# Two RMS norms by chunks of 128 tokens, x in four transfers, and rotation angles behind the next weight split

## The chip, the cores and the metric

The kernel runs on one core of a Trainium2 chip. Its time is the device time of one execution in microseconds; a kernel's time is the median of its runs. The engines are named as in the profile: PE (TensorE), DVE (VectorE), ACT (ScalarE), POOL (GpSimd) and SP (SyncE, which here only issues transfers). Each has its own instruction stream, in program order, and they are held together by semaphores.

## The reference, cut to what matters

Two blocks of a model are applied to 512 tokens of width 1024 in float32. The part that the change touches:

```python
def _rmsnorm(x, g):
    y = xf * lax.rsqrt(jnp.mean(xf * xf, axis=-1, keepdims=True) + NORM_EPS)
    return (y * g.astype(jnp.float32)).astype(x.dtype)

# first block
u = _rmsnorm(h, norm_mix_g[l]);  z = einsum('bsd,dn->bsn', u, w_in[l])      # norm 0
h = h + einsum('bsd,de->bse', merged, w_out[l])
m = _rmsnorm(h, norm_mlp_g[l]);  hid = square(relu(m @ w_mlp_in[l]))        # norm 1
h = h + hid @ w_mlp_out[l];      x = _rmsnorm(h, norm_final_g)

# second block
cos, sin = rope_tables(positions, HEAD_DIM)                                 # rotation angles
lower_bounds = cumsum(softmax(hgrn_lb_logits)) - lb_w[0]
h = rmsnorm(x, norm_mix) * (1.0 + scale_m) + shift_m                        # norm 2
x = x + gate_m * hybrid_mixer(h, cos, sin, ...)
h = rmsnorm(x, norm_ffn) * (1.0 + scale_f) + shift_f
x = x + gate_f * hierarchical_moe(h, ...)
return rmsnorm(x, norm_final)
```

## The kernel before, in words

Tokens lie on the 128 partitions in four chunks (`X[:, c, :]`, c = 0 to 3, 1024 elements each). The large products want the other layout, features on the partitions, so each of the norms 0, 1 and 2 ends in a transposition. Each float32 operand is split into a high and a low part, and one product is three matmuls of 512 columns (`three`, L342 to L344).

Weights come as units of 1 MB in one ring of two buffers (`RAW`, `WH`, `WL`). For each unit, SP issues the load (L519), ACT rounds it to the high part (`split_hi`, L323; it may only begin when PE has finished the unit that used the buffer), DVE subtracts to get the low part (`split_lo`, L327), and PE multiplies. So unit n+1 is split while PE works on unit n. Unit 0 is split outside the loop, on ACT at L671 and on DVE at L951.

A norm before the change goes in steps for all four chunks together. ACT squares each chunk and sums along it (`squares`, L269, a square and the read of the sum); POOL then adds epsilon and raises to -1/2 for the four columns at once (`norm_pool`, L285 and L287); ACT scales chunks 0 and 1 (L274) and DVE chunks 2 and 3 (`norm_scale`, L302); PE transposes (`norm_pe`, L296), eight groups k of 128 features with four transpositions each, into PSUM banks 4 to 7, so that groups 4 to 7 wait for DVE to be done with groups 0 to 3; per group ACT writes the high part `UH` (L279, in norm 2 L281) and DVE the low part `UL` (L310, in norm 2 L312 and L314). After that come PE's products: in norms 0 and 1 the first unit is a `feature` product, which goes over k from 0 to 7 for its first half and then again for its second; each k of the first half of norm 1's unit waits for `UL` of that k.

Norm 1 follows the output projection (units F0 to G0-1). DVE adds its last results chunk by chunk to `X` (L1094), and ACT's squares follow these additions.

After norm 2, ACT computes an exponential for the lower bounds (L788) and then waits for DVE's rotation angles before it computes the sine (L791) and the cosine (L792). Only after these does ACT reach `split_hi` of unit H0+1. DVE has the lower bounds (L1147 to L1150) and the angles (L1153 to L1165) behind the norm and ahead of `split_lo` of unit H0+1. Unit H0 has been split long before.

The last third of the kernel, the experts, is fed by 1 MB loads on SP's queue, each of which waits for a step of the computation that frees its buffer.

Of the kernel before, what the change touches and what calls it, by code (L numbers as in the profile page):

```python
# [81 lines left out]
def build(nc, t):  # L82

    ctx = ExitStack()
    with ctx:
# [178 lines left out]
        def squares(act, j, added, count):  # L264

            for c in range(NC):
                if added is not None:
                    act.wait_ge(added, count + c + 1)
                act.activation(XN[:, c, :], X[:, c, :], ACT.Square, accum_out=SS[:, c:c + 1]).then_inc(norm_sq, 1)  # L269

        def norm_act(act, j, chunks, gain=None):
            act.wait_ge(norm_rs, 2 * j + 2)
            for c in chunks:
                act.activation(XN[:, c, :], X[:, c, :], ACT.Copy, scale=SS[:, 4 + c:5 + c]).then_inc(norm_xn, 1)  # L274
            for k in range(KD):
                act.wait_ge(norm_tr, KD * j + k + 1)
                src = PS[:, 4 + k % 4, :]
                if gain is not None:
                    act.activation(UH[:, k, :], src, ACT.Copy, scale=COLS[:, gain + k:gain + k + 1]).then_inc(norm_hi, 1)  # L279
                else:  # L280
                    act.activation(UH[:, k, :], src, ACT.Identity, scale=MODC[:, 8 + k:9 + k], bias=MODC[:, k:k + 1]).then_inc(norm_hi, 1)  # L281

        def norm_pool(pool, j):
            pool.wait_ge(norm_sq, NC * j + NC)
            pool.tensor_scalar(SS[:, 0:4], SS[:, 0:4], 1.0 / D, EPS, ALU.mult, ALU.add).then_inc(norm_rs, 1)  # L285
            pool.wait_ge(norm_rs, 2 * j + 1)
            pool.tensor_tensor(SS[:, 4:8], SS[:, 0:4], COLS[:, 60:64], ALU.pow).then_inc(norm_rs, 1)  # L287

# [10 lines left out]
        def norm_scale(dve, j, chunks):  # L299
            dve.wait_ge(norm_rs, 2 * j + 2)  # L300
            for c in chunks:
                dve.tensor_scalar(XN[:, c, :], X[:, c, :], SS[:, 4 + c:5 + c], None, ALU.mult).then_inc(norm_xn, 1)  # L302

        def norm_dve(dve, j, gain=None):

            for k in range(KD):
                dve.wait_ge(norm_hi, KD * j + k + 1)
                src, hi = PS[:, 4 + k % 4, :], UH[:, k, :].bitcast(F32)
# [113 lines left out]
        y_out, yc_in = [sem("y_out0"), sem("y_out1")], [sem(f"yc_in{c}") for c in range(NC)]  # L422
# [244 lines left out]
        def _(act):  # L667
            act.wait_ge(const_in, 16 * NCONST)
# [3 lines left out]
            norm_act(act, 0, (0, 1), 0)  # L672
# [94 lines left out]
            norm_act(act, 1, (0, 1), 16)  # L767
# [19 lines left out]
            act.wait_ge(lb, 1)  # L787
            act.activation(LBS[:, 3:6], LBS[:, 0:3], ACT.Exp).then_inc(lb, 1)  # L788

            act.wait_ge(trig, 2)  # L790
            act.activation(SINS, TRG[:, 2, :], ACT.Sin, scale=COLS[:, 53:54]).then_inc(trig, 1)  # L791
            act.activation(COS, TRG[:, 3, :], ACT.Sin).then_inc(trig, 1)  # L792
            for n in range(H0, I0):
                split_hi(act, 0, n // 2, n % 2)
                if n % 2:
                    h = (n - H0) // 2
                    act.wait_ge(unit_done, n + 1)
                    for c in (0, 2):
                        act.activation(V2[:, c:c + 2, HALF * h:HALF * h + HALF], PS[:, 4 * h + c:4 * h + c + 2, :], ACT.Copy).then_inc(z2_out, 1)
# [104 lines left out]
            def h2_row(c):  # L904
                act.wait_ge(norm_rs, 2 * 3 + 2 * c + 2)
# [40 lines left out]
        def _(dve):  # L946
            link = Link(dve, dve_link)
            dve.wait_ge(const_in, 16 * NCONST)
            norm_scale(dve, 0, (2, 3))
# [147 lines left out]
            norm_scale(dve, 1, (2, 3))  # L1097
# [48 lines left out]
            dve.wait_ge(lb, 2)  # L1146
            link(dve.reciprocal(LBS[:, 6:9], LBS[:, 3:6]))  # L1147
            link(dve.tensor_tensor(LBS[:, 3:6], LBS[:, 3:6], LBS[:, 6:9], ALU.mult))
            link(dve.tensor_tensor(LBS[:, 0:3], LBS[:, 3:6], LBS[:, 3:6], ALU.subtract))
            dve.tensor_scalar(LBS[:, 9:12], LBS[:, 0:3], -1.0, 1.0, ALU.mult, ALU.add).then_inc(lb, 1)  # L1150

            dve.wait_ge(pos_in, 32)
            link(dve.tensor_copy(TRG[:, 1, :], TRG[:, 0, :].bitcast(I32)))  # L1153
            link(dve.tensor_scalar(TRG[:, 1, :], TRG[:, 1, :], COLS[:, 52:53], None, ALU.mult))
            for k, quarter in ((2, 0.0), (3, 0.25)):
                if k == 2:
                    dve.wait_ge(x2_d, 4)
                link(dve.tensor_scalar(TRG[:, 0, :].bitcast(I32), TRG[:, 1, :], 1.0 / TWO_PI, quarter, ALU.mult, ALU.add))
                link(dve.tensor_copy(RT, TRG[:, 0, :].bitcast(I32)))
                link(dve.scalar_tensor_tensor(TRG[:, k, :], RT, -TURN[0], TRG[:, 1, :], ALU.mult, ALU.add))  # L1160
                link(dve.scalar_tensor_tensor(TRG[:, k, :], RT, -TURN[1], TRG[:, k, :], ALU.mult, ALU.add))
                link(dve.scalar_tensor_tensor(TRG[:, k, :], RT, -TURN[2], TRG[:, k, :], ALU.mult, ALU.add))
                if quarter:
                    link(dve.tensor_scalar(TRG[:, k, :], TRG[:, k, :], TWO_PI / 4, None, ALU.add))
                dve.tensor_scalar(TRG[:, k, :], TRG[:, k, :], PI_IN, -PI_IN, ALU.min, ALU.max).then_inc(trig, 1)  # L1165
# [344 lines left out]
        def _(pool):  # L1510
            link = Link(pool, pool_link)
            pool.wait_ge(const_in, 16 * NCONST)
            norm_pool(pool, 0)
# [47 lines left out]
            norm_pool(pool, 1)  # L1561
# [66 lines left out]
            def rstd(x):  # L1628
# [3 lines left out]
                pool.wait_ge(norm_rs, 2 * 3 + 2 * x + 1)  # L1632
# [61 lines left out]
        def _(pe):  # L1694
            pe.wait_ge(const_in, 16 * NCONST)
            norm_pe(pe, 0)
# [158 lines left out]
            norm_pe(pe, 1)  # L1855
# [607 lines left out]
```

## Time and profile before

| | |
|---|---|
| median of 3 runs (lowest, highest) | 1414.85 us (1409.91, 1417.54) |
| the profiled execution's own time | 1410.52 us |
| its span | 1408.7 us |
| PE busy | 1295.4 us (92%) |
| DVE, ACT, POOL busy | 643.8, 386.4, 264.6 us |
| mean granted clock of PE | 0.953 |

The span goes from the first instruction to the last. An engine's busy time is the sum over its instructions; matmuls are pipelined, so a matmul's own duration (0.39 us) is longer than the distance to the next (0.23 us). A releaser is the instruction whose semaphore ended a wait. In the rows below a time such as 382.59 is microseconds from the start of the span.

### The profile page before, as it was taken

The page shows a single profiled execution, that of the slowest core. Times are in us where ns is not written, and L with a number is a line of the kernel's source. Part 1 is how long each engine was busy: PE and PEld are TensorE (multiplying, and loading weights), DVE is VectorE, ACT ScalarE, POOL GpSimd, SP SyncE. Part 2 cuts the span into 40 slices and gives each one's busy share as a digit, 9 for nine tenths or more (in the row PEclk, how much of TensorE's full clock was granted, in tenths as well). Part 3 has the DMA queues.
Part 4 walks back from the last instruction along what each step waited for, and adds up shares of the span by engine and source line. Part 5 has one row for each costly group of instructions (what it writes and reads, how often), then busy time and mean ns, then how long its engine had stood idle before and what let it go on. Part 6 is the DMA issues. An engine that isn't in the chain of part 4 may idle for free.

```text
span 1408.7 us, 17535 instructions
## 1 busy us (share of the span) xinstructions
PE 1295.4 (92%) x7287; PEld 998.8 (71%) x7287; DVE 643.8 (46%) x775; ACT 386.4 (27%) x484; POOL 264.6 (19%) x238
## 2 busy tenths in 40 slices
PE   5999999999899999999997899999989879979871
PEld 4888878877788888888884788777867745534440
DVE  3322543256357364563647222238563436434334
ACT  4222445542333231322325232233221400000001
POOL 0320000002011020110200000354342023333212
PEclk9999999999999999999999999998689979999996
DMA  5223333443335255352511322222015879999984
GB/s 215 90 90 104 106 123 124 157 153 109 127 120 209 94 209 206 119 211 111 212 68 62 106 103 90 90 104 92 2 35 199 347 290 415 416 416 417 418 329 187
DMA packets 44340, 249.13 MB, mean 177 GB/s; under 512 B 10181, under 2 KB 10837, under 8 KB 17521
## 3 DMA queue, kind: packets, MB, share of 16 engines
q1 hardware_dynamic: 36514, 228.73, 42.7%
q0 software_dynamic: 7184, 17.35, 3.3%
q10 hardware_dynamic: 576, 2.10, 0.4%
q8 instruction: 50, 0.82, 0.2%
q14 instruction: 16, 0.13, 0.0%
HBM read 240.26 MB, written 17.32 MB: 183 GB/s over the span
## 4 chain that ended last, share of the span: by engine, by line
PE 80%; DMA 7%; DVE 5%; issue 3%; ACT 2%; SPq 1%; POOL 1%; POOLq 0%; DVEq 0%; ACTq 0%
PE ps L342 21%; PE ps L343 20%; PE ps L344 20%; PE ps L2191 5%; PE ps L2209 2%; DMA arena<-in_w_exp 2%; DMA experts<-in_w_exp 2%; PE ps L2035 2%; SPq L586 1%; DVE experts L1250 1%; PE ps L2179 1%; PE ps L296 1%; DMA arena<-h,arena 1%; PE ps L1959 1%; DMA y<-arena 1%
## 5 line engine op out<-in xcount | busy, mean ns | idle before, releaser
L327 DVE TENSOR_TENSOR w_low<-raw,w_high 128x2048 fp32r<-128x2048 f32 x81 | 214.5, 2649 | 289.6 <-ACT w_high L323 289.6
L342 PE MATMUL ps<-u_high,w_high 128*128 128x512 f32 (+1 forms) x712 | 279.0, 392 | 0.0
L343 PE MATMUL ps<-u_low,w_high 128*128 128x512 f32 (+1 forms) x712 | 277.2, 389 | 0.0
L344 PE MATMUL ps<-u_high,w_low 128*128 128x512 f32 (+1 forms) x712 | 277.2, 389 | 0.0
L323 ACT ACTIVATE w_high<-raw 128x2048 fp32r<-128x2048 f32 x81 | 154.6, 1909 | 177.1 <-PE ps L344 148.8
L342 PEld LDWEIGHTS ps<-u_high,w_high 128*128 128x128 f32 (+1 forms) x712 | 132.9, 187 | 30.4 <-issue 1.7
L344 PEld LDWEIGHTS ps<-u_high,w_low 128*128 128x128 f32 (+1 forms) x712 | 132.9, 187 | 28.9
L343 PEld LDWEIGHTS ps<-u_low,w_high 128*128 128x128 f32 (+1 forms) x712 | 132.9, 187 | 28.2 <-issue 0.2
L342 PE MATMUL ps<-w_high,v_high 128*128 128x512 f32 x320 | 125.8, 393 | 2.8 <-POOL v_low L1607 2.8
L343 PE MATMUL ps<-w_low,v_high 128*128 128x512 f32 x320 | 125.0, 391 | 0.0
L344 PE MATMUL ps<-w_high,v_low 128*128 128x512 f32 x320 | 125.0, 391 | 0.0
L1565 POOL TENSOR_TENSOR v_low<-arena,v_high 128x1024 fp32r<-128x1024 f32 x16 | 54.1, 3383 | 265.6 <-ACT v_high L776 265.6
L2191 PE MATMUL ps<-experts,arena 128*64 128x256 f32 x704 | 82.5, 388 | 9.5 <-DMA experts<-in_w_exp 8.5
L342 PE MATMUL ps<-w_high,u_high 128*128 128x512 f32 (+1 forms) x192 | 73.4, 382 | 8.4 <-ACT w_high L323 6.6
L2191 PEld LDWEIGHTS ps<-experts,arena 128*64 128x64 f32 x704 | 52.2, 139 | 33.5 <-issue 9.5
L343 PE MATMUL ps<-w_low,u_high 128*128 128x512 f32 (+1 forms) x192 | 73.2, 381 | 0.0
L344 PE MATMUL ps<-w_high,u_low 128*128 128x512 f32 (+1 forms) x192 | 72.9, 380 | 0.0
L342 PEld LDWEIGHTS ps<-w_high,v_high 128*128 128x128 f32 x320 | 60.4, 189 | 15.8 <-issue 3.5
L930 ACT ACTIVATE arena<-ps 128x128 f32<-128x128 f32 x32 | 8.9, 278 | 225.7 <-PE ps L2191 207.6
L344 PEld LDWEIGHTS ps<-w_high,v_low 128*128 128x128 f32 x320 | 60.4, 189 | 12.8
L343 PEld LDWEIGHTS ps<-w_low,v_high 128*128 128x128 f32 x320 | 60.4, 189 | 12.4
L1438 DVE TENSOR_TENSOR arena<-arena,ps 128x128 f32<-128x128 f32 x32 | 9.2, 288 | 116.7 <-ACT arena L930 76.3
(379 smaller groups left out, 1728.6 us busy)
## 6 DMA issues: line engine op xcount, KB each, us to landing
raw<-in_w SPq DMA_DIRECT2D x82, 1024.0 KB
experts<-in_w_exp SPq DMA_DIRECT2D x69, 1024.0 KB
arena<-in_w_exp SPq DMA_DIRECT2D x30, 1024.0 KB, 20.7
arena<-in_w_ada SPq DMA_DIRECT2D x24, 1024.0 KB
gates<-arena POOLq DMA_DIRECT2D x16, 256.0 KB, 2.3
arena<-gates POOLq DMA_DIRECT2D x2, 2048.0 KB, 9.5
arena<-y SPq DMA_DIRECT2D x8, 512.0 KB, 7.3
x<-in_x SPq DMA_DIRECT2D x1, 2048.0 KB, 7.5
```

The source lines that it names most:

```text
L296: last = pe.transpose(PS[:, b, c * P:(c + 1) * P], XN[:, c, k * P:(k + 1) * P], IDN[:, :])
L323: act.activation(WH[:, 1 - s, :], RAW[:, 1 - s, :], ACT.Copy).then_inc(hi_ready, 1)
L327: dve.tensor_tensor(WL[:, 1 - s, :], RAW[:, 1 - s, :], WH[:, 1 - s, :].bitcast(F32), ALU.subtract).then_inc(lo_ready, 1)
L342: pe.matmul(out, a[0], b[0], start=start, stop=False)
L343: pe.matmul(out, a[0], b[1], start=False, stop=False)
L344: return pe.matmul(out, a[1], b[0], start=False, stop=stop)
L586: sp.dma_start(SLOTS[slot][:, w], e[:, w]).then_inc(gu_in[slot], 16)
L1250: dve.copy_predicated(dst, own, src).then_inc(lvl_a, 1)
L1565: pool.tensor_tensor(VL[:, 2 * s:2 * s + 2, :], SQ[:, s % 2, :, :], VH[:, 2 * s:2 * s + 2, :].bitcast(F32), ALU.subtract).then_inc(hid_lo, 1)
L2035: last = pe.matmul(out[:, hh, P * c:P * c + 64].rearrange("p (n m) -> p n m", m=1 << lev), k_[r, P * c:P * c + P], queries, start=True, st ...
L2191: last = pe.matmul(PS[BLOCK * g:BLOCK * g + BLOCK, bank, 0:256], XT[:, x, P * c + BLOCK * h:P * c + BLOCK * h + BLOCK], SLOTS[slot][:, HAL ...
L2209: last = pe.matmul(PS[BLOCK * g:BLOCK * g + BLOCK, 5 + x, :], HT[:, x, BLOCK * k:BLOCK * k + BLOCK], SLOTS[slot][:, w:w + HALF], start=k = ...
```

## The change

Three things are changed.

Norms 0 and 1 go by chunk. POOL has a pair of instructions on one column for each chunk (`norm_pool_chunk`), each pair as soon as that chunk's square is there. DVE scales all four chunks (ACT none); in norm 1 the scaling of chunk c-1 is put behind the addition of chunk c in DVE's stream. PE transposes chunk by chunk (`norm_pe_chunks`) into eight banks, one for each k, so that no group waits for a bank; in norm 1, where the banks 4 to 7 still hold results that DVE is adding, the transpositions into bank 4+c come with chunk c. Norm 2 keeps its form.

`x` is loaded by four transfers of 512 KB instead of one of 2 MB: chunks 0 and 2 from SP's queue, 1 and 3 from ACT's. A square waits for its own chunk, and all engines still wait for `COLS` and `IDN`, which are now the second and the fourth transfer on SP's queue.

After norm 2, ACT and DVE go straight to the split of unit H0+1. DVE's angles follow its `split_lo` of that unit, the lower bounds that of unit H0+2; ACT's exponential, sine and cosine follow its `split_hi` of unit H0+2.

```diff
+                else:
+                    act.wait_ge(chunk_in[c], 16)
                 act.activation(XN[:, c, :], X[:, c, :], ACT.Square, accum_out=SS[:, c:c + 1]).then_inc(norm_sq, 1)
...
+        def norm_pool_chunk(pool, j, c):
+            pool.wait_ge(norm_sq, NC * j + c + 1)
+            pool.tensor_scalar(SS[:, c:c + 1], SS[:, c:c + 1], 1.0 / D, EPS, ALU.mult, ALU.add).then_inc(norm_rs, 1)
+            pool.wait_ge(norm_rs, 2 * (NC * j + c) + 1)
+            pool.tensor_tensor(SS[:, 4 + c:5 + c], SS[:, c:c + 1], COLS[:, 60:61], ALU.pow).then_inc(norm_rs, 1)
...
+        def norm_pe_chunks(pe, j):
+            for c in range(NC):
+                pe.wait_ge(norm_xn, NC * j + c + 1)
+                for k in range(KD):
+                    if j and k > 4 + c:
+                        continue
+                    late = j and k == 4 + c
+                    for x in range(c + 1) if late else (c,):
+                        last = pe.transpose(PS[:, k, x * P:(x + 1) * P], XN[:, x, k * P:(k + 1) * P], IDN[:, :])
+                    if c == NC - 1:
+                        last.then_inc(norm_tr, 1)
...
         def norm_scale(dve, j, chunks):
-            dve.wait_ge(norm_rs, 2 * j + 2)
             for c in chunks:
+                dve.wait_ge(norm_rs, 2 * (NC * j + c) + 2)
                 dve.tensor_scalar(XN[:, c, :], X[:, c, :], SS[:, 4 + c:5 + c], None, ALU.mult).then_inc(norm_xn, 1)
...
-            sp.dma_start(X[:, :, :], t["x"]).then_inc(const_in, 16)
+            sp.dma_start(X[:, 0, :], t["x"][:, 0, :]).then_inc(chunk_in[0], 16)
             sp.dma_start(COLS[:, :], t["cols"]).then_inc(const_in, 16)
+            sp.dma_start(X[:, 2, :], t["x"][:, 2, :]).then_inc(chunk_in[2], 16)
             sp.dma_start(IDN[:, :], t["ident"]).then_inc(const_in, 16)
...
+            for c in (1, 3):
+                act.dma_start(X[:, c, :], t["x"][:, c, :]).then_inc(chunk_in[c], 16)
...
-            norm_act(act, 1, (0, 1), 16)
+            norm_act(act, 1, (), 16)
...
-            act.wait_ge(lb, 1)
-            act.activation(LBS[:, 3:6], LBS[:, 0:3], ACT.Exp).then_inc(lb, 1)
-
-            act.wait_ge(trig, 2)
-            act.activation(SINS, TRG[:, 2, :], ACT.Sin, scale=COLS[:, 53:54]).then_inc(trig, 1)
-            act.activation(COS, TRG[:, 3, :], ACT.Sin).then_inc(trig, 1)
             for n in range(H0, I0):
                 split_hi(act, 0, n // 2, n % 2)
+                if n == H0 + 1:
+                    act.wait_ge(lb, 1)
+                    act.activation(LBS[:, 3:6], LBS[:, 0:3], ACT.Exp).then_inc(lb, 1)
+                    act.wait_ge(trig, 2)
+                    act.activation(SINS, TRG[:, 2, :], ACT.Sin, scale=COLS[:, 53:54]).then_inc(trig, 1)
+                    act.activation(COS, TRG[:, 3, :], ACT.Sin).then_inc(trig, 1)
...
-            norm_scale(dve, 0, (2, 3))
+            norm_scale(dve, 0, range(NC))
...
                         dve.tensor_tensor(xs, xs, PS[:, 4 * h + c, :], ALU.add).then_inc(wo_add, 1)
+                        if h and c:
+                            norm_scale(dve, 1, (c - 1,))
...
             for n in range(H0, J0 + 3):
                 split_lo(dve, 0, n // 2, n % 2)
+                if n == H0:
+                    angles()
+                elif n == H0 + 1:
+                    lower_bounds()
```

## Rows read from the trace of the kernel before

**Rows 1.** PE's waits from 20 us on: total us, times, longest us.
```profile
PE ps L296 <- ACT arena L274: 9.1, 2, 5.6
```
**Rows 2.** The chain of work that ended last, opening: start us, us, what.
```profile
1.64 7.26 DMA ident<-in_ident
8.92 4.26 ACT arena L269 x8
...
14.98 2.09 ACT arena L274 x2
```
**Rows 3.** Timeline of the opening: start us, us, instruction, idle before it.
```profile
16.12 2.28 DVE L951 TENSOR_TENSOR w_low<-raw,w_high 128x2048 fp32r<-128x2048 f32 x1
17.20 5.87 PE L296 MATMUL ps<-ident,arena 128*128 128x128 f32 x32 [17.20 <-ACT arena L274]
...
19.05 5.98 DVE L310 SCALAR_TENSOR_TENSOR u_low<-ps,cols,u_high 128x512 fp32r<-128x512 f32 x8 [0.65 <-ACT u_high L279]
...
22.83 0.48 PE L342 MATMUL ps<-u_high,w_high 128*128 128x512 f32 x1
```
**Rows 4.** Timelines of POOL and DVE, where POOL works on one column.
```profile
1105.84 0.22 POOL L1631 TENSOR_SCALAR sumsq<-sumsq 128x1 f32<-128x1 f32 x1 [1.75 <-ACT experts L902]
1106.14 0.57 POOL L1633 TENSOR_TENSOR sumsq<-sumsq,cols 128x1 f32<-128x1 f32 x1
...
1400.58 1.23 DVE L1504 TENSOR_TENSOR x<-x,arena 128x1024 f32<-128x1024 f32 x1
...
1400.70 1.52 POOL L1633 TENSOR_TENSOR sumsq<-sumsq,cols 128x1 f32<-128x1 f32 x1
```
**Rows 5.** Timeline of norm 1 on ACT, DVE and PE.
```profile
378.70 0.19 ACT L269 ACTIVATION_READ_ACCUMULATOR arena<-x 128x1 f32 x1
...
380.35 1.42 DVE L302 TENSOR_SCALAR arena<-x,sumsq 128x1024 f32<-128x1024 f32 x2 [2.56 <-POOL sumsq L287]
...
382.59 5.90 PE L296 MATMUL ps<-ident,arena 128*128 128x128 f32 x32 [5.61 <-ACT arena L274]
...
384.46 5.95 DVE L310 SCALAR_TENSOR_TENSOR u_low<-ps,cols,u_high 128x512 fp32r<-128x512 f32 x8 [2.70 <-ACT u_high L279]
...
388.24 0.48 PE L342 MATMUL ps<-u_high,w_high 128*128 128x512 f32 x1
```
**Rows 6.** Windows: us, busy (x) of PE, PEld, DVE, ACT, POOL, granted clock, DMA share, GB/s.
```profile
384.00:386.00 2.00, 2.00 (x11) 2.00 (x10) 1.44 (x2) 1.67 (x3) 0.00 (x0) 0.50 0.03 8
776.00:780.00 4.00, 1.03 (x3) 0.87 (x4) 3.43 (x2) 2.34 (x2) 0.00 (x0) 0.50 0.10 16
```
**Rows 7.** Timeline behind norm 2 on ACT, DVE and PE.
```profile
761.75 1.28 ACT L788 ACT_TABLE_LOAD   x1
...
765.07 0.42 DVE L1153 CAST arena<-arena 128x512 f32<-128x512 int32 x1
...
773.04 0.43 DVE L1165 TENSOR_SCALAR arena<-arena 128x512 f32<-128x512 f32 x1
...
774.65 3.69 ACT L323 ACTIVATE w_high<-raw 128x2048 fp32r<-128x2048 f32 x2
...
776.57 4.49 DVE L327 TENSOR_TENSOR w_low<-raw,w_high 128x2048 fp32r<-128x2048 f32 x2 [3.11 <-ACT w_high L323]
...
778.97 0.76 PE L342 MATMUL ps<-w_high,u_high 128*128 128x512 f32 x1 [6.59 <-ACT w_high L323]
...
783.38 0.39 PE L342 MATMUL ps<-w_high,u_high 128*128 128x512 f32 x1
...
786.11 0.39 PE L342 MATMUL ps<-w_high,u_high 128*128 128x512 f32 x1
```
**Rows 8.** The chain of work that ended last, in the experts.
```profile
1307.93 29.80 DMA arena<-in_w_exp
```
**Rows 9.** Windows again, first and last of three, in the second block's mixer.
```profile
1000.00:1020.00 20.00, 19.50 (x232) 16.35 (x228) 10.30 (x14) 6.55 (x10) 5.92 (x7) 0.81 0.01 2
...
1040.00:1060.00 20.00, 15.51 (x136) 12.21 (x134) 10.30 (x15) 6.83 (x11) 7.79 (x8) 0.83 0.21 78
```

More of the change, by code:

```diff
@@ L268, in squares, with norm_bank @@
                     act.wait_ge(added, count + c + 1)
+                else:
+                    act.wait_ge(chunk_in[c], 16)
                 act.activation(XN[:, c, :], X[:, c, :], ACT.Square, accum_out=SS[:, c:c + 1]).then_inc(norm_sq, 1)
+        def norm_bank(j, k):
+            return k if j < 2 else 4 + k % 4
         def norm_act(act, j, chunks, gain=None):
-            act.wait_ge(norm_rs, 2 * j + 2)
+            if chunks:
+                act.wait_ge(norm_rs, RS_MIX)
             for c in chunks:
@@ L276, in norm_act @@
                 act.wait_ge(norm_tr, KD * j + k + 1)
-                src = PS[:, 4 + k % 4, :]
+                src = PS[:, norm_bank(j, k), :]
                 if gain is not None:
@@ L281, in norm_act @@
                     act.activation(UH[:, k, :], src, ACT.Identity, scale=MODC[:, 8 + k:9 + k], bias=MODC[:, k:k + 1]).then_inc(norm_hi, 1)
+        RS_MIX = 4 * NC + 2
+        def norm_pool_chunk(pool, j, c):
[3 more added lines that the diff above has]
+            pool.tensor_tensor(SS[:, 4 + c:5 + c], SS[:, c:c + 1], COLS[:, 60:61], ALU.pow).then_inc(norm_rs, 1)
         def norm_pool(pool, j):
@@ L307, in norm_dve @@
                 dve.wait_ge(norm_hi, KD * j + k + 1)
-                src, hi = PS[:, 4 + k % 4, :], UH[:, k, :].bitcast(F32)
+                src, hi = PS[:, norm_bank(j, k), :], UH[:, k, :].bitcast(F32)
                 if gain is not None:
@@ L421, in build @@
         over_step, over_x, over_y, over_in = [sem("overflow_" + x) for x in ("steps", "x_in", "y_out", "weights_in")]
-        y_out, yc_in = [sem("y_out0"), sem("y_out1")], [sem(f"yc_in{c}") for c in range(NC)]
+        y_out, chunk_in = [sem("y_out0"), sem("y_out1")], [sem(f"chunk_in{c}") for c in range(NC)]
         fin_x, fin_d = sem("final_x"), sem("final_done")
@@ L639, in _ @@
                 for k in range(2):
-                    sp.dma_start(YC[:, c, k, :], t["y"][S * k + P * c:S * k + P * c + P, :]).then_inc(yc_in[c], 16)
+                    sp.dma_start(YC[:, c, k, :], t["y"][S * k + P * c:S * k + P * c + P, :]).then_inc(chunk_in[c], 16)
             for c in range(NC):
@@ L671, in _ @@
             act.activation(WH[:, 0, :], RAW[:, 0, :], ACT.Copy).then_inc(hi_ready, 1)
-            norm_act(act, 0, (0, 1), 0)
+            norm_act(act, 0, (), 0)
             for n in range(A0, V0):
@@ L904, in h2_row @@
             def h2_row(c):
-                act.wait_ge(norm_rs, 2 * 3 + 2 * c + 2)
+                act.wait_ge(norm_rs, RS_MIX + 2 * c + 2)
                 act.activation(H2[:, c, :], X[:, c, :], ACT.Copy, scale=SS[:, 4 + c:5 + c]).then_inc(h2_d, 1)
@@ L1094, in _ @@
                         dve.tensor_tensor(xs, xs, PS[:, 4 * h + c, :], ALU.add).then_inc(wo_add, 1)
+                        if h and c:
+                            norm_scale(dve, 1, (c - 1,))
             dve.wait_ge(c_act, 1)
             dve.tensor_tensor(CA[:, :], CA[:, :], COLS[:, 24:32], ALU.mult).then_inc(c_act, 1)
-            norm_scale(dve, 1, (2, 3))
+            norm_scale(dve, 1, (3,))
             norm_dve(dve, 1, 16)
@@ L1144, in _ @@
             norm_dve(dve, 2)
[L1146 to L1165, printed above, removed]
+            def angles():
+                dve.wait_ge(pos_in, 32)
+                link(dve.tensor_copy(TRG[:, 1, :], TRG[:, 0, :].bitcast(I32)))
+                link(dve.tensor_scalar(TRG[:, 1, :], TRG[:, 1, :], COLS[:, 52:53], None, ALU.mult))
+                for k, quarter in ((2, 0.0), (3, 0.25)):
+                    if k == 2:
+                        dve.wait_ge(x2_d, 4)
+                    link(dve.tensor_scalar(TRG[:, 0, :].bitcast(I32), TRG[:, 1, :], 1.0 / TWO_PI, quarter, ALU.mult, ALU.add))
+                    link(dve.tensor_copy(RT, TRG[:, 0, :].bitcast(I32)))
+                    link(dve.scalar_tensor_tensor(TRG[:, k, :], RT, -TURN[0], TRG[:, 1, :], ALU.mult, ALU.add))
+                    link(dve.scalar_tensor_tensor(TRG[:, k, :], RT, -TURN[1], TRG[:, k, :], ALU.mult, ALU.add))
+                    link(dve.scalar_tensor_tensor(TRG[:, k, :], RT, -TURN[2], TRG[:, k, :], ALU.mult, ALU.add))
+                    if quarter:
+                        link(dve.tensor_scalar(TRG[:, k, :], TRG[:, k, :], TWO_PI / 4, None, ALU.add))
+                    dve.tensor_scalar(TRG[:, k, :], TRG[:, k, :], PI_IN, -PI_IN, ALU.min, ALU.max).then_inc(trig, 1)
@@ L1166, in _, with lower_bounds @@
+            def lower_bounds():
+                dve.wait_ge(lb, 2)
+                link(dve.reciprocal(LBS[:, 6:9], LBS[:, 3:6]))
+                link(dve.tensor_tensor(LBS[:, 3:6], LBS[:, 3:6], LBS[:, 6:9], ALU.mult))
+                link(dve.tensor_tensor(LBS[:, 0:3], LBS[:, 3:6], LBS[:, 3:6], ALU.subtract))
+                dve.tensor_scalar(LBS[:, 9:12], LBS[:, 0:3], -1.0, 1.0, ALU.mult, ALU.add).then_inc(lb, 1)
             for n in range(H0, J0 + 3):
                 split_lo(dve, 0, n // 2, n % 2)
+                if n == H0:
+                    angles()
+                elif n == H0 + 1:
+                    lower_bounds()
@@ L1301, in choose @@
                 for c in range(c0, c0 + 2):
-                    dve.wait_ge(norm_rs, 2 * 3 + 2 * c + 2)
+                    dve.wait_ge(norm_rs, RS_MIX + 2 * c + 2)
                     dve.wait_ge(logits, c + 1)
@@ L1498, in finish @@
             def finish(c):
-                dve.wait_ge(norm_rs, 2 * 3 + 2 * NC + 2 * c + 2)
+                dve.wait_ge(norm_rs, RS_MIX + 2 * NC + 2 * c + 2)
                 dve.scalar_tensor_tensor(X[:, c, :], X[:, c, :], SS[:, 4 + c:5 + c], ROW_F, ALU.mult, ALU.mult).then_inc(fin_d, 1)
             for c in range(NC):
-                dve.wait_ge(yc_in[c], 32)
+                dve.wait_ge(chunk_in[c], 48)
                 link(dve.tensor_tensor(X[:, c, :], X[:, c, :], YC[:, c, 0, :], ALU.add))
@@ L1512, in _ @@
             pool.wait_ge(const_in, 16 * NCONST)
-            norm_pool(pool, 0)
+            for c in range(NC):
+                norm_pool_chunk(pool, 0, c)
             pool.wait_ge(late_in, 16 * NLATE)
@@ L1560, in _ @@
             pool.dma_start(ACC[0:1, :], t["b_ada"]).then_inc(b_in, 16)
-            norm_pool(pool, 1)
+            for c in range(NC):
+                norm_pool_chunk(pool, 1, c)
             with pool.Fori(0, 4) as gi:
@@ L1631, in rstd @@
                 pool.tensor_scalar(SS[:, c:c + 1], SS[:, c:c + 1], EPS, None, ALU.add).then_inc(norm_rs, 1)
-                pool.wait_ge(norm_rs, 2 * 3 + 2 * x + 1)
+                pool.wait_ge(norm_rs, RS_MIX + 2 * x + 1)
                 pool.tensor_tensor(SS[:, 4 + c:5 + c], SS[:, c:c + 1], COLS[:, 60:61], ALU.pow).then_inc(norm_rs, 1)
@@ L1695, in _ @@
             pe.wait_ge(const_in, 16 * NCONST)
-            norm_pe(pe, 0)
+            norm_pe_chunks(pe, 0)
             for n in range(A0, V0):
@@ L1854, in _ @@
                 tokens(pe, n % 2, U, 4 * kh, 4 * h, wo_chunk, kh == 0, kh == 1)
-            norm_pe(pe, 1)
+            norm_pe_chunks(pe, 1)
             def mlp(gi):
```

4 lines of the change are left out of this document (2 added, 2 removed).

## The prediction

> **What bounds the kernel now.** I read the waits of PE first, since PE is busy 92% of the span and carries most of the chain of work that ended last. Apart from the experts' stage, PE waits long in few places: for the scaled x ahead of the transpositions of norms 1 and 2 (9.1 us in two waits [rows 1]), and 6.59 us for a weight split [rows 7]. The same kind of wait lies in the opening. Between these places it works without a gap, so a gain at them reaches PE's next unit in full. I then read the timelines of the three places.
>
> In the opening the chain goes from the transfer of `IDN` (landed at 8.90) over the squares (to 13.18), unit 0's high part on ACT, and ACT's scaling (14.98 to 17.07) [rows 2]. PE starts to transpose at 17.20 and multiplies at 22.83 [rows 3]. In norm 1 the last square ends at 378.89, DVE begins to scale at 380.35, PE transposes from 382.59 and multiplies at 388.24 [rows 5]. Behind norm 2, ACT is free at 761.75 but sits in a table load and a wait for the angles, which DVE computes from 765.07 to 773.47; the splits follow, and PE, idle for 6.59 us, takes up unit H0+1 at 778.97 [rows 7].
>
> **Part 1, angles behind the split.** After the change ACT splits unit H0+1 from 761.75 to about 763.7 (two splits take 3.69, so about 1.9 each). DVE ends the norm shortly before 765.07, and its low part takes 2.3 (two take 4.49), so it is ready near 766.8 [rows 7]. PE needs it at 778.97 - 6.59 = 772.38. The wait goes whole: 6.6 us.
>
> The stall has a second price. At 776 to 780 the granted clock is 0.50, that is 1.2 GHz instead of 2.4 [rows 6], after PE's idle time; the first 12 matmuls of unit H0+1 take 783.38 - 778.97 = 4.41 us and the next 12 take 2.73 [rows 7]. Without the gap the clock has no reason to fall there: another 1.7 us. Sum 8.3, and 6.6 if the clock falls all the same.
>
> What is late next? DVE's angles (8.4 us) run from 766.8 to 775.2, then the low part of unit H0+2, whose high part ACT has by 772.4 + 1.9 = 774.3, is ready at 777.5. PE wants it after one unit, 48 matmuls of 2.73/12 us or 10.9 us, at 783.3. Cover of 5.8 us. ACT's exponential, sine and cosine with two table loads come behind 775.2 and end near 778.5, ahead of the copies at 783.3. Behind the moved angles only this one split is queued. The loads on SP's queue wait for splits that come earlier than now. These moves I cost at nothing.
>
> **Part 2, norm 1.** The last square ends at 378.89 as before [rows 5]. POOL's pair on one column takes 0.22 and 0.57, 0.87 with the gap between, when nothing disturbs it, so it ends at 379.85; beside a DVE operation the power took 1.52 [rows 4]. But DVE is free for 2.56 us before 380.35, and the scaling of chunk 2 lies early in that stretch. I take 0.87. DVE scales one chunk (1.42 for two, so 0.7) from 379.95 to 380.7. Of the 32 transpositions 21 belong to chunks 0 to 2 and lie in the wait; the 11 with chunk 3 begin at 380.8. From PE's first transposition to DVE's first low part it took 384.46 - 382.59 = 1.87, with four slow transpositions (0.85, below) in it where there is one now, so I estimate 1.15: DVE begins at 381.95, ends the first low part at 382.7, and PE multiplies at about 382.8 instead of 388.24.
>
> Then DVE sets the pace: eight low parts take 5.95 [rows 5], more than PE's 24 matmuls at 0.227, 5.45. The first half of the unit ends at 381.95 + 5.95 + 0.7 = 388.6 instead of 388.24 + 5.5 = 393.7. Gain 5.1.
>
> The lower bound comes from the clock. Before, it was 0.50 at 384 to 386 [rows 6], and the 32 transpositions took 5.90 us. If it stays there for the first 3.4 us of the new products (at half speed twice the 1.7 that unit H0+1 lost), 24 matmuls lose up to 1.7 us. Now PE transposes inside the former gap, so I take none of it. Range 3.4 to 5.3.
>
> DVE's new waits stand in its stream ahead of the next addition: the addition of chunk c+1 comes one chunk of PE's work (12 matmuls, 2.73 us) behind that of chunk c. By then the square (1.25) and POOL's pair (1.0) of chunk c are done or all but done, and the scaling (0.7) is over before the addition after that. If a margin is used up, chunk 1 or 2 is late, but chunk 3, which decides, has only the last addition ahead of it, on which all of this rests already.
>
> **Part 3, norm 0.** Squares end at 13.18 as before if `IDN` lands at 8.90. Chunks are then ready one by one from 11.9, the last at 15.0 with POOL undisturbed (13.18 + 0.1 + 0.87 + 0.1 + 0.75). Squares come 1.07 us apart [rows 2]. Here DVE's scalings do lie beside POOL's next pair: if each of them holds POOL up until it ends, the last chunk is ready at 16.3.
>
> The Trainium skill, page "SBUF — State Buffer", section "SBUF: two separate sides", says that DVE and GpSimd share one pair of ports under an exclusive lock, and that the loser blocks for the whole instruction. The trace agrees (0.57 us alone, 1.52 beside DVE [rows 4]). By this rule the later of the two ends would hold in norm 0.
>
> DVE then has unit 0's low part, 2.28 [rows 3], still ahead of `UL`: it ends at 17.3 or 18.6. On PE, 32 transpositions took 5.87 here and 5.90 in norm 1 at a granted clock of 0.50 [rows 3, 5, 6], so I read the start of PE as slow too, at about 0.21 us each (four banks in 0.85). From 12.0 on, the first 24 need until about 17.1, and DVE could begin the first low part of chunk 3's k = 0 near 18.3 (17.1 and 1.2). Both lead to a first low part at about 19.1 and a product at 19.2 instead of 22.83. Again DVE paces it: last `UL` at 18.4 + 5.98 = 24.4, the half ends at 25.1 instead of 28.3. Gain 3.2, between 1.9 (port lock and slow PE both) and 4.4 (neither).
>
> The four transfers: `IDN`, 64 KB behind 2 MB, took 7.26 us from issue to landing [rows 2]. `IDN` still stands behind 1 MB on SP's queue and shares the engines with ACT's 1 MB. If ACT's half runs beside SP's, `IDN` lands as before; if it comes behind, at most about 1 us earlier; the later issue (one more transfer of about 0.45 ahead of it) could cost 0.4. I take 0.
>
> **The sum.** 8.3 + 5.1 + 3.2 = 16.6 us: 1410.5 becomes 1393.9 for an execution like the profiled one. The median of the runs shown is 4.3 higher, so I forecast 1414.85 - 16.6 = 1398.2. The experts' stage is bound by loads (the chain waits 29.8 us for one [rows 8]), but each load there is issued behind a step of the computation, so I let the whole stage move along. The bounds give 6.6 + 3.4 + 1.5 = 11.5 and 8.4 + 5.3 + 5.4 = 19.1.
>
> **Rivals.**
>
> *Held up by lock and clock.* POOL blocked in norm 0 (1.9 instead of 3.2), slow products behind norm 1 (3.4), the clock falling at H0+1 anyway (6.6): 11.9 us, 1403. For it: [rows 4, 6]. Against: DVE is idle where norm 1's last pair runs, and PE is fed without a gap at H0. 13%.
>
> *The gain is lost in the experts.* If the weight stream ran freely there, its loads would end when they end now, and so would the kernel: 1414.9. Against it: every load waits for a buffer that the computation frees. 5%.
>
> *Angles push the low part of H0+2 out.* It decides once DVE is over 5.8 us later than I reckon, and costs what is above. A doubling of the angles (8.4 us) would leave 1401. 3%.
>
> *Slower: the clock in the attention of the second block.* From 1000 to 1060 us PE runs many small products at a mean granted clock of 0.81 to 0.83 in the first and last of three stretches of 20 us, with 19.5 and 15.5 us busy [rows 9], so about 53 in the three; the clock is a mix of 0.5 and 1. The same kernel would start that stage 17 us earlier, in another state of the clock. At 0.82 some 64% of the 53 busy us, 34 us, are at the full clock; if all of it fell to half, it would lose 34 us against 17 gained: 1432. It decides from 17 us of such work on. Against it: PE's pattern of work there is untouched. 2%.
>
> **How the numbers follow.** Forecast 1398.2, 77% with its own spread (1393 to 1402). The runs shown differ by 7.6 us, so the low end is 1396 less half of that, about 1392; the high end takes in the first rival, 1405.5. A change of 0.5% (7 us) is about what a measurement of this kernel can tell from none: faster 0.92 (forecast, first and third rival), same 0.06, slower 0.02.
>
> **What would show it.** Part 1: no wait of PE for `w_high` behind norm 2, and the clock at 1.00 there. Part 2: a first product about 3.9 us behind the last square's end (now 9.35). Part 3: PE's first product near 19.2 and one POOL pair of 0.9 us per chunk; pairs of 1.5 us mean the lock. The distance from the start of unit H0+2 to the end unchanged means that nothing was lost behind. A new wait of PE for `w_low` at H0+2, or a shorter start with an unchanged end, would make it wrong.

## The result, and the profile after

| | before | after |
|---|---|---|
| median of the first runs | 1415.62 us (4 runs) | 1394.76 us (1389.74 to 1397.56, 4 runs) |
| ratio to before, 95% interval | | 0.9848 (0.9822 to 0.9875) |
| the profiled execution, span | 1410.52, 1408.7 | 1397.56, 1395.7 |
| POOL instructions, busy | 238, 264.6 us | 250, 269.3 us |

The kernel became 20.9 us faster; 16.6 had been forecast. The two profiled executions differ by only 13 us. That is no contradiction, as the control below shows: two executions of one kernel differ by several us, and here a long one of the new kernel stands beside a short one of the old.

The opening of the changed kernel, timeline of DVE, POOL, ACT and PE (start us, us, instruction, idle before it). It answers to [rows 3] and [rows 4].

```profile
12.32 0.75 DVE L328 TENSOR_SCALAR arena<-x,sumsq 128x1024 f32<-128x1024 f32 x1 [0.45 <-POOL sumsq L295]
13.78 0.75 DVE L328 TENSOR_SCALAR arena<-x,sumsq 128x1024 f32<-128x1024 f32 x1 [0.71 <-POOL sumsq L295]
15.25 0.75 DVE L328 TENSOR_SCALAR arena<-x,sumsq 128x1024 f32<-128x1024 f32 x1 [0.71 <-POOL sumsq L295]
15.92 2.28 DVE L980 TENSOR_TENSOR w_low<-raw,w_high 128x2048 fp32r<-128x2048 f32 x1
18.12 5.35 DVE L336 SCALAR_TENSOR_TENSOR u_low<-ps,cols,u_high 128x512 fp32r<-128x512 f32 x8
...
12.37 0.75 POOL L293 TENSOR_SCALAR sumsq<-sumsq 128x1 f32<-128x1 f32 x1
13.20 0.55 POOL L295 TENSOR_TENSOR sumsq<-sumsq,cols 128x1 f32<-128x1 f32 x1
13.83 0.75 POOL L293 TENSOR_SCALAR sumsq<-sumsq 128x1 f32<-128x1 f32 x1
14.67 0.55 POOL L295 TENSOR_TENSOR sumsq<-sumsq,cols 128x1 f32<-128x1 f32 x1
...
12.93 0.18 ACT L271 ACTIVATION_READ_ACCUMULATOR arena<-x 128x1 f32 x1
...
12.02 5.76 PE L311 MATMUL ps<-ident,arena 128*128 128x128 f32 x32 [12.02 <-DVE arena L328]
19.01 0.47 PE L368 MATMUL ps<-u_high,w_high 128*128 128x512 f32 x1 [1.23 <-DVE u_low L336]
```

PE's first product is at 19.01 instead of 22.83. What is late next is DVE: from 15.25 on it scales the last chunk, makes the low part of unit 0 and the first low part of the norm without a gap. PE's 32 transpositions run without a gap from 12.02 too, but ACT's first high part behind them is ready at 17.74, 0.4 us before DVE is free for the low part. POOL's first operation takes 0.75 us each time that a scaling of DVE has begun just before it, and ends with it.

Norm 1 and the stretch behind norm 2 in the changed kernel, timelines again, beside [rows 5] and [rows 7]:

```profile
376.45 0.19 ACT L271 ACTIVATION_READ_ACCUMULATOR arena<-x 128x1 f32 x1
...
376.72 0.19 POOL L293 TENSOR_SCALAR sumsq<-sumsq 128x1 f32<-128x1 f32 x1 [1.89 <-ACT arena L271]
377.00 0.55 POOL L295 TENSOR_TENSOR sumsq<-sumsq,cols 128x1 f32<-128x1 f32 x1
...
377.58 0.75 DVE L328 TENSOR_SCALAR arena<-x,sumsq 128x1024 f32<-128x1024 f32 x1 [1.39 <-POOL sumsq L295]
379.47 5.36 DVE L336 SCALAR_TENSOR_TENSOR u_low<-ps,cols,u_high 128x512 fp32r<-128x512 f32 x8 [1.14 <-ACT u_high L285]
...
753.44 1.91 ACT L349 ACTIVATE w_high<-raw 128x2048 fp32r<-128x2048 f32 x1
763.75 1.92 ACT L349 ACTIVATE w_high<-raw 128x2048 fp32r<-128x2048 f32 x1 [8.40 <-PE ps L370]
...
774.57 1.94 ACT L828 ACTIVATE arena<-ps 128x1024 f32<-128x1024 f32 x2 [4.83 <-PE ps L370]
...
756.65 2.28 DVE L353 TENSOR_TENSOR w_low<-raw,w_high 128x2048 fp32r<-128x2048 f32 x1
...
767.18 2.29 DVE L353 TENSOR_TENSOR w_low<-raw,w_high 128x2048 fp32r<-128x2048 f32 x1
```

The chain of waits has PE's first product of norm 1 3.7 us behind the last square's end (376.64), where it was 9.35:

```profile
380.24 0.14 issue
380.37 0.47 PE ps L368
```

Unit H0+1 is split as soon as the norm is done, its low part is ready at 758.9, and PE ends unit H0 only at 763.7, where ACT's next split begins. The low part of unit H0+2 is ready at 769.5; PE wants it at about 774.6, when ACT copies the results of H0+1. PE's waits from 20 us on, beside [rows 1], no longer hold one for `w_high`. Of the two waits of [rows 1] the one in norm 2 (3.5 us) is left, now 3.7; norm 1 has 1.0 and 0.6 instead of 5.6:

```profile
PE ps L322 <- ACT arena L280: 3.7, 1, 3.7
...
PE ps L311 <- DVE arena L328: 1.0, 1, 1.0
...
PE ps L368 <- DVE u_low L336: 0.6, 1, 0.6
```

The clock behind norm 2, windows of the changed kernel (us, busy (x) of PE, PEld, DVE, ACT, POOL, granted clock, DMA share, GB/s), beside the second of [rows 6]:

```profile
760.00:764.00 4.00, 4.00 (x20) 3.30 (x19) 3.79 (x8) 0.25 (x1) 0.00 (x0) 1.00 0.72 264
764.00:768.00 4.00, 4.00 (x19) 3.32 (x18) 3.83 (x7) 3.95 (x4) 0.00 (x0) 1.00 0.00 0
```

### The profile page after: what moved, and what is told of

It is laid out like the page before. It is cut to its first block, busy times and chain, and to the rows that moved or that the text cites. A ratio compares the mean times of both kernels' runs of the same rounds, so it can differ in the third digit from the quotient of the medians.

```text
span 1395.7 us, 17551 instructions
## 1 busy us (share of the span) xinstructions
PE 1299.5 (93%) x7287; PEld 1002.0 (72%) x7287; DVE 644.1 (46%) x779; ACT 381.6 (27%) x480; POOL 269.3 (19%) x250
## 4 chain that ended last, share of the span: by engine, by line
PE 81%; DMA 7%; DVE 5%; issue 3%; ACT 2%; POOL 1%; SPq 1%; POOLq 0%; DVEq 0%; ACTq 0%
PE ps L368 21%; PE ps L370 21%; PE ps L369 21%; PE ps L2231 5%; DMA experts<-in_w_exp 4%; PE ps L2249 3%; PE ps L2075 2%; PE ps L2219 1%; DVE experts L1288 1%; DMA arena<-h,arena 1%; DMA y<-arena 1%; SPq L613 1%; PE ps L1976 1%; PE ps L1999 1%; PE ps L1807 1%
## 5 line engine op out<-in xcount | busy, mean ns | idle before, releaser
L349 ACT ACTIVATE w_high<-raw 128x2048 fp32r<-128x2048 f32 x81 | 154.7, 1910 | 186.5 <-PE ps L370 158.7
```

What stands on the lines that cost most here:

```text
L349: act.activation(WH[:, 1 - s, :], RAW[:, 1 - s, :], ACT.Copy).then_inc(hi_ready, 1)
```

## The experiments

The theory: the three parts remove PE's waits, their gains add up and reach the end whole, and part of the gain is the clock that fell in a wait. The rivals were a clock that falls all the same, a gain lost behind, and POOL blocked by DVE.

**Each part alone.** The kernel before with one part of the diff: the angles, norm 1, or norm 0 with the four transfers.

The angles (e1):

```diff
             for n in range(H0, J0 + 3):
                 split_lo(dve, 0, n // 2, n % 2)
+                if n == H0:
+                    angles()
+                elif n == H0 + 1:
+                    lower_bounds()
```

> The kernel before with the angles part alone (exponential, sine, cosine and DVE's angles and lower bounds behind the next splits). Theory: the gains add up, and this one is the wait of PE for w_high (6.6 us) and the half-clock start of unit H0+1 (1.7 us): 8.3 us, ratio 0.9941, with no wait of PE for w_high behind norm 2. Rival (the clock falls there whatever is done): 6.6 us, ratio 0.9953. Rival (part of the gain comes back as a wait for w_low at H0+2): 3 us or less.

Norm 1 (e2), with `norm_pool_chunk` and `norm_scale` by chunk for it:

```diff
-            norm_pe(pe, 1)
+            norm_pe_chunks(pe, 1)
```

> The kernel before with norm 1 alone by chunk. Theory: PE's first product of unit G0 comes 3.6 to 3.9 us behind the last square's end instead of 9.35, a gain of 5.1 to 5.8 us, ratio 0.9959 to 0.9964, and the granted clock stays at 1.00 in the gap. Rival (clock falls in the gap): gain 3.4 to 4, with a window at 0.50 around the first products.

Norm 0 (e3), likewise, and x in four transfers:

```diff
-            norm_pe(pe, 0)
+            norm_pe_chunks(pe, 0)
```

> The kernel before with norm 0 alone by chunk and x in four transfers. Theory: PE's first product near 19.0 us instead of 22.8 us, every later split 3.8 us earlier until the clock differs; ratio 0.9973. The part of it that the gates of the second mixer or of the attention give back or add by another phase of the clock changes from run to run, both ways. Rival (shift of the start is eaten by the clock each time): PE's splits behind 300 us only 2.3 us earlier, ratio 0.9984.

| | median, runs | ratio (95%) |
|---|---|---|
| angles only | 1404.79, 7 | 0.9931 (0.9905 to 0.9957) |
| norm 1 only | 1404.84, 11 | 0.9939 (0.9916 to 0.9961) |
| norm 0 only | 1410.24, 12 | 0.9968 (0.9947 to 0.9990) |

The product of the three is 0.9839, and all parts together gave 0.9848: within the intervals they add up. The angles part alone leaves PE no wait for `w_high`, and none for `w_low` came up at H0+2. In norm 1 alone the first product comes 3.74 us behind the last square's end, as expected, and the clock stays at 1.00 through the former gap, in which PE now transposes (its windows; columns as above):

```profile
378.00:380.00 2.00, 1.53 (x13) 1.06 (x10) 0.61 (x3) 0.93 (x2) 0.74 (x2) 1.00 0.03 8
380.00:382.00 2.00, 1.31 (x11) 1.19 (x11) 0.86 (x2) 0.95 (x2) 0.00 (x0) 1.00 0.00 0
```

Its median, though, lies 10.8 us below the kernel before where 5.1 to 5.8 were expected (the ratio's interval just reaches them), and the table of stages below finds only 5.7 in norm 1. Its 11 runs have a mean clock of 0.954 against 0.948; the half-clock time that went in norm 1 (6.8 us) is 0.0024 of that. Where the rest lies its one profile doesn't show.

**The control.** The kernel before, unchanged; there is no diff.

> The kernel before, unchanged. Theory: its runs differ by several us because PE's clock falls at other moments, so over the runs the span goes with the mean granted clock: a run whose clock is 0.005 higher is some 7 us shorter. Rival (the difference is in the loads of the experts): spans differ at the same clock.

1415.25 us (10 runs), ratio 1.0002 (0.9981 to 1.0023). The 29 other runs of the kernel before that were measured beside these four kernels go from 1409.34 to 1421.26 us, and their mean granted clock from 0.953 to 0.943. Ordered by clock, they are almost ordered by time: the lowest clocks, 0.943 and 0.944, have 1421.26 and 1420.9, the highest, twice 0.953, have 1409.34 and 1409.7. A line through the 29 has 1.17 us for each 0.001 of clock, with a correlation of -0.97. This speaks for the theory and against the loads: runs of one kernel differ by how long PE is at half the clock.

**The stage by stage table.** With such differences single stages are better compared than ends. The starts of ACT's splits (L323 or L349 and so on, one for each unit) divide the trace. Length of each stretch in the profiled executions, in us; "old" are those in which the part in question is as before:

| stretch | old | new |
|---|---|---|
| start to unit 22 (norm 0 in it) | 278.2, 278.5, 278.6, 278.6, 278.1 | 274.3, 274.6, 274.9, 274.4, 274.4, 274.8 |
| unit 22 to G0 (attention) | 84.9 to 89.7 in all, whatever the kernel | |
| G0 to G0+2 (norm 1) | 36.5 to 36.8 in each of six | 30.9 in each of six |
| G0+2 to H0 | 323.1 in all | |
| H0 to H0+6 (norm 2, angles) | 99.5, 102.7, 101.2, 102.7, 102.6, 101.2 | 92.6, 90.2, 91.1, 90.6 |
| H0+6 to unit 78 | 114.5 or 114.6 in all | |
| unit 78 to 81 (mixer) | 146.4 to 153.2 in all, whatever the kernel | |
| unit 81 to the end (experts) | 320.2 to 322.3 in all | |

Left out are the kernels with filler work, with DVE held and with norm 2 by chunk, each in the stretch that it alters.

Gains: 3.8 in norm 0, 5.7 in norm 1, 101.7 - 91.1 = 10.6 behind norm 2, 20.1 together, against 20.9 of the medians. Of the 10.6, about 0.6 lies ahead of unit H0's first product, where the angles part does nothing: from that product to the split of H0+6 the six old executions take 64.7 to 66.3 us, 65.7 on average, and the four new ones 55.6 to 56.4, 55.8 on average, so 9.9 is what the moved angles are worth. The stretch up to the end of the experts has not grown, so nothing is given back there. The attention and the mixer vary by 5 and 7 us from execution to execution, and the longer ones have the lower mean clock. The profiled execution of the changed kernel had 151.6 in the mixer where [rows 9] belong to one with 147.1; its windows show the lower clock:

```profile
1000.00:1020.00 20.00, 17.43 (x184) 15.03 (x186) 13.27 (x21) 1.87 (x4) 7.64 (x9) 0.74 0.00 1
1020.00:1040.00 20.00, 18.49 (x192) 15.70 (x192) 10.45 (x20) 5.45 (x9) 7.67 (x9) 0.74 0.16 54
```

**The changed kernel in more runs,** unchanged, so again without a diff.

> The changed kernel, unchanged, in more runs. Theory: the spans of its runs go with the mean granted clock as those of the kernel before do (about 1.1 us for each 0.001), and the mean clock of many runs lies above the one of before, since the half-clock stretches in norm 1 and at unit H0+1 are gone; ratio 0.985 to 0.988. Rival (the higher clock in the first four runs was chance): mean clock equal to that of before, 0.948, and ratio 0.988 or above.

1394.71 us (6 runs), ratio 0.9853 (0.9830 to 0.9877). Mean clock 0.954 here and 0.955 in the first four runs, against 0.948 for before (29 runs). The rival falls. The traces show where the clock rose. The stretch with norm 1 has a mean granted clock of 0.91 in the profile of each of six old executions (6.8 us at half the clock) and 1.00 in each of six new ones; the stretch behind norm 2 has 0.88 to 0.93 in six old ones and 0.93 to 0.96 in four new ones, on average 20.5 us at half the clock against 9.4. Together 18 us less at half the clock are 0.0064 of the mean clock, which is the whole rise. By the line above this is 7 us, an estimate: about a third of the 20.9 (a share of it, not in addition). PE was idle for part of this time, so it is likely less.

**The price of the stall through the clock.** The kernel before, with work that nobody reads in PE's wait for unit H0+1:

```diff
             for n in range(H0, J0 + 6):
+                if n == H0 + 1:
+                    pe.wait_ge(norm_lo, KD * 3)
+                    for k in range(24):
+                        pe.matmul(PS[:, 7, :], IDN[:, :], XN[:, 0, 0:512], start=True, stop=True)
                 unit_is_in(pe, n)
```

> The kernel before, with 24 matmuls of 512 columns that nobody reads in PE's wait for the split of unit H0+1. Theory (the stall has a second price through the clock): the clock stays at 1.00 there, unit H0+1 begins at the same distance from the end of norm 2 as before, and its first 12 matmuls take 2.7 us instead of 4.4. Rival (a start after any wait for weights is slow): 4.4 us with the clock at 1.00.

Its timeline of PE, and one of its windows:

```profile
771.12 20.76 PE L1890 MATMUL ps<-arena,ident 128*128 128x512 f32 x48
791.31 0.79 PE L342 MATMUL ps<-w_high,u_high 128*128 128x512 f32 x1
...
794.45 0.39 PE L342 MATMUL ps<-w_high,u_high 128*128 128x512 f32 x1
```

```profile
776.00:780.00 4.00, 4.00 (x10) 1.74 (x10) 3.53 (x2) 2.24 (x2) 0.00 (x0) 1.00 0.15 20
```

The plain float32 matmuls were longer than I had reckoned (48 records, 0.43 us apart), so the unit began 12 us late, at 791.31, the expectation of the same start fell, and the execution took 1422.29 us (one run). The rest held in the main: the clock stayed at 1.00, and the first 12 matmuls took 794.45 - 791.31 = 3.1 us, not 4.4 (2.7 expected), the first of them 0.64 alone. The filler took away the fall of the clock and the wait with it, so this run doesn't part the two. The traces with the wait do: the unit's matmuls are 0.43 us apart only as long as the granted clock is 0.50, and 0.23 from its rise on, in the middle of the unit. In the control the same place was dearer than in the profile of [rows 7]: the wait 7.6 us, and the first 12 matmuls 784.02 - 778.77 = 5.25 us. Timeline of PE and two windows of the control:

```profile
778.77 0.77 PE L342 MATMUL ps<-w_high,u_high 128*128 128x512 f32 x1 [7.59 <-ACT w_high L323]
...
784.02 0.39 PE L342 MATMUL ps<-w_high,u_high 128*128 128x512 f32 x1
```

```profile
780.00:784.00 4.00, 4.00 (x10) 3.06 (x10) 0.86 (x1) 0.00 (x0) 0.00 (x0) 0.50 0.88 365
784.50:787.00 2.50, 2.50 (x12) 2.05 (x11) 0.00 (x0) 0.00 (x0) 0.00 (x0) 1.00 0.33 138
```

The other four old executions are like the control: wait and first 12 matmuls 7.6 and 5.0 to 5.3 us.

**POOL beside DVE.** The changed kernel, with DVE's scalings of norm 0 held until all four roots are there:

```diff
-                dve.wait_ge(norm_rs, 2 * (NC * j + c) + 2)
+                dve.wait_ge(norm_rs, 2 * (NC * j + c) + 2 if j else 2 * NC)
```

> The changed kernel, with DVE's scalings in norm 0 held until POOL has all four roots. Theory (POOL is blocked by DVE's scaling): POOL's pairs take 0.19 and 0.55 us each with nothing of 0.75 or 0.89 among them, and the last root is there 0.85 to 1.0 us behind the last square instead of 2.1. Rival (a pair on one column is slow whenever pairs follow each other): durations of 0.75 and 0.89 stay.

Timeline of its opening on ACT, POOL and DVE:

```profile
12.99 0.19 ACT L271 ACTIVATION_READ_ACCUMULATOR arena<-x 128x1 f32 x1
...
13.27 0.19 POOL L293 TENSOR_SCALAR sumsq<-sumsq 128x1 f32<-128x1 f32 x1 [0.21 <-ACT arena L271]
13.54 0.55 POOL L295 TENSOR_TENSOR sumsq<-sumsq,cols 128x1 f32<-128x1 f32 x1
...
14.21 2.74 DVE L328 TENSOR_SCALAR arena<-x,sumsq 128x1024 f32<-128x1024 f32 x4 [14.21 <-POOL sumsq L295]
```

All eight of POOL's operations take 0.19 or 0.55 us, and the last root is there at 14.09, 0.92 behind the last square; with DVE beside it, it was 15.22 - 13.11 = 2.1. That a scaling of DVE holds POOL up is shown, and it costs the last root 1.2 us. Holding DVE is no gain, though: its four scalings in a row end at 16.95 instead of 16.00, PE's first product comes at 21.08 instead of 19.01, and the stretch to unit 22 takes 276.4 us instead of 274.3 to 274.9 (the one run's 1394.60 us doesn't show it, within the spread). The Trainium skill, page "SBUF — State Buffer", section "Who interferes with whom", says that of a DVE instruction in a two-port mode and a GpSimd instruction the one that starts first holds the shared ports for its whole length and the other is blocked. The trace agrees (0.75 and 0.89 beside a scaling, 0.19 and 0.55 without); no run here shows the mode of the scaling.

**The four transfers.** The kernel of the norm 0 part, with x in one transfer again:

```diff
-            sp.dma_start(X[:, 0, :], t["x"][:, 0, :]).then_inc(chunk_in[0], 16)
+            sp.dma_start(X[:, :, :], t["x"]).then_inc(const_in, 16)
             sp.dma_start(COLS[:, :], t["cols"]).then_inc(const_in, 16)
-            sp.dma_start(X[:, 2, :], t["x"][:, 2, :]).then_inc(chunk_in[2], 16)
...
-            for c in (1, 3):
-                act.dma_start(X[:, c, :], t["x"][:, c, :]).then_inc(chunk_in[c], 16)
```

> The kernel before with norm 0 by chunk and x still in one transfer of 2 MB. Theory (the four transfers give nothing, since all engines wait for IDN behind the same bytes): squares start at 8.9 us and PE's first product comes near 19.0 us as with four transfers. Rival (the four transfers are part of the gain): squares or the first product 0.3 us or more later than with four.

Timeline of its opening on ACT and PE:

```profile
8.88 1.06 ACT L269 ACTIVATE arena<-x 128x1024 f32<-128x1024 f32 x1 [6.89 <-DMA ident<-in_ident]
...
19.11 0.47 PE L366 MATMUL ps<-u_high,w_high 128*128 128x512 f32 x1 [0.89 <-DVE u_low L334]
```

In the five profiles with four transfers (DVE not held) the squares begin at 8.85 to 9.16 and PE multiplies at 19.01 to 19.54; with one transfer the squares begin at 8.79 to 8.92 in six profiles. The four transfers give nothing and may cost 0.1 us: the squares still wait for `IDN`, behind the same bytes.

**The angles put back into the changed kernel,** and ACT's exponential, sine and cosine ahead of its `split_hi` (these lines are left out below).

```diff
+            lower_bounds()
+            angles()
             for n in range(H0, J0 + 3):
                 split_lo(dve, 0, n // 2, n % 2)
-                if n == H0:
-                    angles()
-                elif n == H0 + 1:
-                    lower_bounds()
```

> The changed kernel with the angles, bounds, sine and cosine put back ahead of the split of unit H0+1. Theory (the parts add up, and the angles part is worth its wait of 6.6 us and two to four us of clock): the stretch from the split of unit H0 to the split of unit H0+6 takes 99 to 103 us instead of 90 to 91, ratio to before 0.992. Rival (with norms 0 and 1 changed the angles part is worth its wait alone): 97 us.

1401.96 us, ratio 0.9903 (0.9873 to 0.9934). The stretch from H0 to H0+6 took 101.2 us (one profile): the angles part is worth about 10 us with and without the others, and the rival with 97 falls.

**A version that beats both.** Norm 2 by chunk too, in all eight banks, on top of the change:

```diff
         def norm_bank(j, k):
-            return k if j < 2 else 4 + k % 4
+            return k
...
-            norm_pool(pool, 2)
+            for c in range(NC):
+                norm_pool_chunk(pool, 2, c)
...
-            norm_pe(pe, 2)
+            norm_pe_chunks(pe, 2)
```

> The changed kernel, with norm 2 by chunk as well: POOL's pair per chunk, ACT scales each chunk when its root is there, PE transposes chunk by chunk into eight banks. Theory: ACT's last scaling ends 1.3 us earlier, and PE's unit H0 no longer queues behind transpositions that wait for banks, so unit H0 ends 3 to 4 us earlier and so does the kernel; ratio to before 0.983. Rival (DVE's low parts, 1.18 us for each k, set the end of unit H0): 1.3 us.

Timeline of ACT and PE, and a window:

```profile
735.11 4.25 ACT L279 ACTIVATE arena<-x,sumsq 128x1024 f32<-128x1024 f32 x4
...
744.06 0.47 PE L367 MATMUL ps<-w_high,u_high 128*128 128x512 f32 x1 [1.50 <-DVE u_low L339]
```

```profile
744.00:748.00 4.00, 3.78 (x10) 2.42 (x11) 3.89 (x7) 4.00 (x6) 0.00 (x0) 0.68 0.49 205
```

1389.88 us (1386.89 to 1392.32, 6 runs), ratio to before 0.9817 (0.9794 to 0.9840): 4.8 us below the changed kernel's 1394.71, of which the stretch from H0 to H0+6 shows 2.1 (88.5 against 90.2, 91.1 and 90.6). The expectation of 3 to 4 holds for the start of unit H0 and not for its end. ACT scales without a wait for POOL, and PE's first product of H0 (744.06, just behind the first low part) comes 30.8 us behind the split of H0, where it was 34.5 to 34.9. But half of that is lost again in unit H0: its first products come at the pace of DVE's low parts, as the rival had it, and then at half the clock (0.68 in the window). Where the other 2.7 us of the medians are I can't say from one profile; its runs have a mean clock of 0.957, so part of it may be clock, which was not separated.

## Why the prediction was right, and where it was off

The range of 1392 to 1405.5 held the measured 1394.76, 3.4 below the forecast of 1398.2. The mechanism was right, but each part was priced too low: the gain of 20.9 us (17.7 to 25.2 by the ratio's interval; 20.1 by stages) lies above the 19.1 that the bounds gave, and the range held it because half the spread of the runs had been added to it. That much is luck. (The sum of the bounds also doesn't use part 3's own 1.9 and 4.4 but 1.5 and 5.4, of which no working stands there.) The parts:

- **Angles behind the split**, forecast 8.3, measured 9.9 from unit H0's first product on (10.6 in the whole stretch). The wait went whole, nothing queued behind the angles became late (the low part of H0+2 was ready 5 us early, forecast 5.8), and the clock stayed up. Both terms were too small, since I took them from one execution: wait 6.6 and clock 1.7 us, where the control and four others have 7.6 and 2.3 to 2.5. The six old executions have 101.7 on average where the profiled one had 99.5. It was the most favourable of the six.
- **Norm 1**, forecast 5.1, measured 5.7. The first product came 3.7 us behind the last square's end in each of six profiles (forecast 3.9), and POOL's pair was undisturbed there, as argued from DVE's idle time.
- **Norm 0**, forecast 3.2, measured 3.8; first product at 19.01 (forecast 19.2). Both bounds that I gave for the first low part proved close: POOL was held up by DVE, and the first 20 of the 32 transpositions were 0.21 us apart (the rest 0.11: the prediction put 5.87 us for 32 and 0.21 for one side by side, which don't agree). In both norms the loss that I subtracted for DVE's pace (0.4 us here, 0.3 in norm 1) did not come: eight low parts took 5.35 us in the changed kernel instead of 5.98 [rows 3], 0.66 apart, as fast as PE's three matmuls (0.68). That the spacing of low parts stays as it was is the step that failed. It was read as DVE's own pace, but before it was PE's: ACT's high parts, for which DVE's low parts wait, came 0.85 us apart as long as each waited for four slow transpositions (timeline of ACT in the kernel before, below), and the last low parts were 0.66 apart already then. In the changed kernel the high parts come 0.57 to 0.59 apart, so only DVE's 0.66 is left.

```profile
18.33 0.69 ACT L279 ACTIVATE u_high<-ps,cols 128x512 fp32r<-128x512 f32 x1 [1.27 <-PE ps L296]
19.18 0.69 ACT L279 ACTIVATE u_high<-ps,cols 128x512 fp32r<-128x512 f32 x1 [0.17 <-PE ps L296]
20.04 0.69 ACT L279 ACTIVATE u_high<-ps,cols 128x512 fp32r<-128x512 f32 x1 [0.17 <-PE ps L296]
```

- **The tail moved along.** The experts took 320.2 to 322.3 us in every kernel, though they wait for loads.

Of the rivals, the lock is real and was within the bounds of norm 0. The clock falling in norm 1 or at H0+1 all the same was not seen in any changed profile. The slower rival, a mixer at half the clock, exists as a spread of 7 us that all kernels show, not as 34 us.

## What to carry to other kernels

Look at the places where the main engine waits, and price each by what the clock does in them, too: a wait of 6.6 to 7.6 us here cost 9 to 10. Take that price from several executions, since one may be a lucky one. Side work that is needed late belongs behind the step that the next product waits for, and a reduction in front of a transposition can be cut into chunks, so that only the last chunk is left when the last input comes.

## What the runs showed of the hardware that I had not expected

Executions of the kernel before differ by 12 us (0.8%), and the mean granted clock nearly orders them: 1.17 us for each 0.001 over 29 runs. The clock is at 0.50 in stretches whose place in the attention and the mixer changes from execution to execution, while all stages of dense matmuls repeat within 0.1 us. In the opening the windows give the granted clock as 1.00, yet the transpositions run there as in norm 1 before: the first 19 or 20 are 0.21 us apart, the rest 0.11. In norm 1 this turn comes at 386.5, where the granted clock rises from 0.50 to 1.00; in the opening it comes at 21.3 (16.3 in the changed kernel), so PE was most likely at half the clock until then, and the 1.00 of the windows does not show it. It also means that the 5.87 and 5.90 us of [rows 3, 5] are a mixture of both levels; 32 transpositions at 1.00 throughout take 3.71 us (the version with norm 2 by chunk).
